# The border from ffn_down to dil_in by halves of tokens, and dil_in's first group with its value columns second

## What is computed

```python
# first block, its end
h = rms_norm(x, g_ffn_pre[l])
x = x + rms_norm(swiglu(h, w_gate_up[l], w_down[l]), g_ffn_post[l])
# second block, its start (rms_norm_2 is the same norm)
h = rms_norm_2(x, mixer_norm[layer])
proj = (h @ w_in).reshape(B, S, ATTN_N_GROUPS, 3, ATTN_HEADS_PER_GROUP, ATTN_HEAD_DIM)
for g, (window, dilation) in enumerate(ATTN_GROUPS):
    q = rms_norm_2(proj[:, :, g, 0], q_gain[g]) * scale
    k = rms_norm_2(proj[:, :, g, 1], k_gain[g])
    o, lse = dilated_window_attention(q, k, proj[:, :, g, 2], window, dilation)
```

## Time and profile before

| | us |
|---|---|
| median of three runs | 1457.39 |
| lowest and highest | 1456.97, 1458.7 |
| the profiled execution, device time | 1458.71 |
| the profiled execution, first to last instruction | 1456.9 |

### The profile page before, as it was taken

How to read it: one execution, slowest core, us unless ns; L and a number is a source line. 1 busy time by engine, 2 the same in 40 slices (tenths; PEclk the granted TensorE clock), 3 DMA queues, 4 the chain that set the end, 5 groups by cost and what they waited for, 6 DMA issues and landing times.

```text
span 1456.9 us, 22944 instructions
## 1 busy us (share of the span) xinstructions
PE 1443.8 (99%) x8638; PEld 1223.7 (84%) x8638; DVE 958.1 (66%) x1475; ACT 641.8 (44%) x1000; POOL 345.9 (24%) x313
## 2 busy tenths in 40 slices
PE   9999999999999999999999999999999999999999
PEld 6888779898899888888999788888888888888787
DVE  6524673566628665547877787737666867767878
ACT  6222675453345322222555542433665333335554
POOL 0200102020021743543000564555422110110000
PEclk9999999999999999999999999999999999999999
DMA  5622103422034898786745123222203333334543
GB/s 178 199 91 88 58 2 117 145 87 88 1 87 147 285 311 307 283 279 262 259 137 191 58 87 112 91 88 87 60 2 87 86 102 100 86 106 152 197 152 123
DMA packets 170779, 195.91 MB, mean 134 GB/s; under 512 B 8636, under 2 KB 136636, under 8 KB 167876
## 3 DMA queue, kind: packets, MB, share of 16 engines
q1 hardware_dynamic: 164036, 168.49, 36.5%
q0 software_dynamic: 5600, 26.24, 4.6%
q10 hardware_dynamic: 1056, 0.00, 0.0%
HBM read 169.52 MB, written 25.19 MB: 134 GB/s over the span
## 4 chain that ended last, share of the span: by engine, by line
PE 95%; DVE 3%; ACT 1%; issue 0%; DMA 0%; POOL 0%; SPq 0%; POOLq 0%; DVEq 0%; ACTq 0%
PE ps L2510 27%; PE ps L2512 27%; PE ps L2511 27%; PE ps L2963 3%; PE ps L3052 2%; PE ps L3070 1%; PE ps L3150 1%; PE ps L3159 1%; PE ps L2973 1%; PE ps L658 1%; DVE w_lo L2240 1%; ACT w_hi L1492 0%; PE ps L2994 0%; PE ps L3218 0%; PE ps L3219 0%
## 5 line engine op out<-in xcount | busy, mean ns | idle before, releaser
L2510 PE MATMUL ps<-a_hi,w_hi 128*128 128x512 f32 (+2 forms) x1708 | 608.1, 356 | 5.5 <-issue 2.8
L2512 PE MATMUL ps<-a_hi,w_lo 128*128 128x512 f32 (+2 forms) x1708 | 603.1, 353 | 0.0
L2511 PE MATMUL ps<-a_lo,w_hi 128*128 128x512 f32 (+2 forms) x1708 | 602.9, 353 | 0.0
L2510 PEld LDWEIGHTS ps<-a_hi,w_hi 128*128 128x128 f32 (+1 forms) x1708 | 322.9, 189 | 54.3 <-issue 7.0
L2512 PEld LDWEIGHTS ps<-a_hi,w_lo 128*128 128x128 f32 (+1 forms) x1708 | 322.8, 189 | 45.1
L2511 PEld LDWEIGHTS ps<-a_lo,w_hi 128*128 128x128 f32 (+1 forms) x1708 | 322.9, 189 | 44.4 <-issue 0.7
L1124 ACT ACTIVATE w_hi<-raw 128x2048 fp32r<-128x2048 f32 x94 | 179.7, 1912 | 172.4 <-PE ps L2512 172.4
L1702 DVE TENSOR_TENSOR w_lo<-raw,w_hi 128x2048 fp32r<-128x2048 f32 x75 | 176.1, 2348 | 87.5 <-ACT w_hi L1124 87.1
L2211 DVE TENSOR_TENSOR arena<-ps,rstd 128x512 f32<-128x512 f32 x88 | 59.6, 687 | 124.9 <-PE ps L2512 119.8
L2510 PE MATMUL ps<-w_hi,a_hi 128*128 128x512 f32 x346 | 135.6, 392 | 1.7 <-DVE w_lo L2240 1.4
L2512 PE MATMUL ps<-w_hi,a_lo 128*128 128x512 f32 x346 | 134.8, 390 | 0.0
(11 more groups left out here) (290 smaller groups left out, 1782.9 us busy)
## 6 DMA issues: line engine op xcount, KB each, us to landing
raw<-in_w_gate_up SPq DMA_DIRECT2D x44, 512.0 KB, 5.2
raw<-in_ffn_w_up SPq DMA_DIRECT2D x44, 512.0 KB, 4.5
raw<-in_attn_w_in SPq DMA_DIRECT2D x36, 512.0 KB, 4.2
raw<-in_w_in SPq DMA_DIRECT2D x24, 512.0 KB, 4.7
arena<-in_ffn_w_down SPq DMA_DIRECT2D x24, 512.0 KB, 6.0
arena<-in_w_down POOLq DMA_DIRECT2D x22, 512.0 KB, 6.8
sums_dram<-arena POOLq DMA_DIRECT2D x11, 1024.0 KB, 4.2
sums_dram<-arena SPq DMA_DIRECT2D x11, 1024.0 KB, 4.2
```

What stands on the lines that cost most here:

```text
L2510: pe.matmul(dst, s_hi, m_hi, start=start, stop=False, skip_group_check=across)
L2511: pe.matmul(dst, s_hi, m_lo, start=False, stop=False, skip_group_check=across)
L2512: return pe.matmul(dst, s_lo, m_hi, start=False, stop=stop, skip_group_check=across)
```

## The change

**In ffn_down.** The last two steps put their weights into the two halves of slot 1, so slot 0 is free for dil_in after step 25 (before: after step 27); step 27 now waits for step 24, and step 28 for step 26. The norm of the later 256 tokens (half 1) is taken inside the last run: PE sums in front of step 24 (`post_sum(1)`), ACT takes the root behind its work for step 26, DVE inverts in front of its work for step 27 (`factor_of_half`), PE spreads in front of step 25 (`post_spread(1)`), and DVE, ACT and DVE scale, add, round and subtract by feature tile and half (`post_scaled`, `post_hi`, `post_lo`), in 256 columns. POOL adds nothing to x any more. `stay_clocked` is gone.

**At the border.** PE starts with the first two tiles of dil_in for half 1, eight feature tiles of six 256-column matmuls, as each becomes ready; then come two blocks of the values' first chunk for half 1, the two tiles for half 0, and the values' other two blocks (`dil_opening`).

**In dil_in.** The first group's chunks come in the order 0, 4, 5, 1, 2, 3. Its tiles lie in banks 0, 1, 0, 1, 2, 3, 6, 7, so tile 2 needs tile 0's bank and tile 3 tile 1's. The sum of the squares for `mixer_2` and the first two averages move into chunk 5 (`mixer_means`). DVE scales the values between tiles 1 and 2. ACT's list for the first group is written anew.

```diff
-                self.w, self.half = self.g % 2, (c - PAIRS_K) // 2 % 2
+                last_two = c >= DOWN_STEPS - 2
+                self.w = DOWN_0 % 2 if last_two else self.g % 2
+                self.half = c - (DOWN_STEPS - 2) if last_two else (c - PAIRS_K) // 2 % 2
+                self.w_free = c - (2 if c < PAIRS_K + 2 or c == DOWN_STEPS - 1 else 3 if last_two else 4) + 1
...
+        DIL_ORDER = ((0, 4, 5, 1, 2, 3), tuple(range(6)), tuple(range(6)))
...
         def tile_bank(grp, t):
 
-            return (6, 7, 0, 1)[t - 4] if grp == 0 and t >= 4 else t % 4
+            return (0, 1, 0, 1, 2, 3, 6, 7)[t] if grp == 0 else t % 4
...
             def dil_chunk(grp, c):
-                ch = Chunk(G["dil_in"], grp, 6, c)
+                ch = dil_at(grp, c)
                 if ch.first_of_gemm:
                     pool.wait_ge(norms["mixer_2"].added, 3)
                     squares_split(0)
                     return
+                if ch.second_of_gemm:
+                    return
                 split_lo(ch)
-                if ch.second_of_gemm:
+                if grp == 0 and c == 5:
                     squares_split(1)
                 if c < 4:
                     squares_split(8 * grp + 2 * c)
...
+            post_hi(1, 2)
+            ch = Chunk(G["ffn_down"], 0, 2, DOWN_STEPS - 1)
+            act.wait_ge(raw_loaded[ch.next_slot], ch.next_loads)
+            act.wait_ge(tile_done, G["ffn_down"].signal0 + DOWN_STEPS - 3)
+            act.activation(w_hi[:, ch.next_slot, :], raw[:, ch.next_slot, :], ACT.Copy).then_inc(weights_hi, 1)
             act.wait_ge(mask_ready, 10)
+            post_hi(1, 3), post_hi(1, 4)
...
+            post_hi(1, 5)
             split_hi(Chunk(G["dil_in"], 0, 6, 0))
+            post_hi(1, 6), post_hi(1, 7)
+            root_of_half(0)
...
+                if grp == 0:
+                    if c == 0:
+                        square(0), square_top(0), square(1)
+                        split_hi(dil_at(0, 5))
+                        mixer_norm_out()
+                        square_top(1)
+                        root(0)
+                    elif c < 4:
+                        split_hi(ch)
+                        square(2 * c), square_top(2 * c)
+                        root(2 * c - 1)
+                        square(2 * c + 1), square_top(2 * c + 1)
+                        root(2 * c)
+                    return
...
+            def halves_of_residual():
+
+                post_lo(1, 2), post_scaled(1, 3)
+                split_here(Chunk(G["ffn_down"], 0, 2, DOWN_STEPS - 1))
+                for k in range(3, KT):
+                    if k > 3:
+                        post_scaled(1, k)
+                    post_lo(1, k)
+                factor_of_half(0)
+                split_here(Chunk(G["dil_in"], 0, 6, 0))
+                post_scaled(0, 0)
+                for k in range(KT):
+                    if k + 1 < KT:
+                        post_scaled(0, k + 1)
+                    post_lo(0, k)
...
+                elif t.c == RUNS[2] + 4:
+                    post_scaled(1, 0), post_scaled(1, 1), post_lo(1, 0), post_scaled(1, 2), post_lo(1, 1)
+            halves_of_residual()
+            half_sum("mixer_2", KT + 4)
+            split_here(Chunk(G["dil_in"], 0, 6, 1))
...
+                chunk_ready(tiles)
+                half(1)
+                post_spread(0)
+                chunk_ready(values)
+                pe.wait_ge(norms["ffn_post"].sq, 6)
+                value_blocks((2, 3))
+                half(0)
+                value_blocks((0, 1)).then_inc(tile_done, 2)
...
-            summed(norms["ffn_post"], "dil_in")
...
+                    pe.wait_ge(freed["dve"], ch.freed + (j + 1) - (2 if grp == 0 or grp == 1 and c < 2 else 0))
...
-                    elif t >= 1 and not ch.second_of_gemm:
+                    if grp == 0 and t >= 3 or grp and t >= 1 or grp == 1:
                         head_mean(8 * grp + (t - 1), t - 1)
```

More of the change, by code:

```diff
@@ L2840, in seven_products, with post_sum @@
                         pe.sem_inc(tile_done, 1)
+            def post_sum(h):
+                norm = norms["ffn_post"]
+                pe.wait_ge(product_joined, 5)
+                pe.wait_ge(norm.added, CREDIT + (7, 5)[h])
+                blocks = (2 * h, 2 * h + 1)
+                for b in blocks:
+                    last = pe.matmul(ps[:, 4, b:b + 1], square_sum[:, b * 128:(b + 1) * 128], ones[:, 0:1],
+                                     start=b == blocks[0], stop=h == 1, skip_group_check=True)
+                if h == 0:
+                    for f in range(4):
+                        pe.wait_ge(norm.sq, 4 + f // 2)
+                        for b in blocks:
+                            last = pe.matmul(ps[:, 4, b:b + 1], token_squares(1)[:, f, b * 128:b * 128 + 128], ones[:, 0:1],
+                                             start=False, stop=f == 3, skip_group_check=True)
+                last.then_inc(norm.sum, 1)
@@ new lines, in post_spread, with dil_opening, half, value_blocks @@
+            def post_spread(h):
+                norm = norms["ffn_post"]
+                pe.wait_ge(norm.inverse, 2 * (1 - h) + 2)
+                pe.matmul(ps[:, POST_FACTOR[h], 0:256], ones[:, :], diagonal[:, HALVES[h]], start=True, stop=True)\
+                  .then_inc(norm.spread, 1)
+            def dil_opening():
+                tiles, values = dil_at(0, 0), dil_at(0, 4)
+                ready = norms["mixer_2"].ready
+                whi, wlo = weights(tiles.slot, KT)
+                vhi, vlo = weights(values.slot, 4)
+                def half(h):
+                    for k in range(KT):
+                        pe.wait_ge(ready, (1 - h) * KT + k + 1)
+                        for j in range(2):
+                            cols = slice(j * 128, j * 128 + 128)
+                            last = three(ps[:, j, HALVES[h]], (whi[:, k, cols], wlo[:, k, cols]),
+                                         (a_hi[:, k, HALVES[h]], a_lo[:, k, HALVES[h]]), k == 0, k == KT - 1, across=True)
+                            if h == 0 and k == KT - 1:
+                                last.then_inc(tile_done, 1)
+                        if h == 1 and k == 4:
+                            post_sum(0)
+                    return last
+                def value_blocks(blocks):
+                    for b in blocks:
+                        tok = slice(b * 128, b * 128 + 128)
+                        for k in range(4):
+                            last = three(ps[:, value_banks(0)[b], :], (a_hi[:, k, tok], a_lo[:, k, tok]),
+                                         (vhi[:, k, :], vlo[:, k, :]), k == 0, False, across=True)
+                    return last
+                chunk_ready(tiles)
[6 more added lines that the diff above has]
+                value_blocks((0, 1)).then_inc(tile_done, 2)
```

201 lines of the change are left out of this document (96 added, 105 removed).

## The result

The changed kernel takes **1462.96 us** (median of seven runs, 1462.07 to 1463.97) against 1457.78 (seven runs, 1456.97 to 1458.70) for the kernel before: **5.2 us more**, ratio 1.0036 with a 95% interval of 1.0024 to 1.0048. The forecast was 1460.5, slower by 3.1 than the median of three runs that it started from. The profiled execution took 1462.71 with a span of 1460.9, 4.0 more than the one before. The other 1.2 us is a matter of which execution was profiled: the one before was the slowest of its seven, the one after among the faster.

The account below looks back on a forecast made before the run. The prediction took PE, busy 1443.8 of 1456.9 us, as the bound: 7.1 us won at the border, 10.3 lost in two waits (6.2 and 4.1), so +3.1 on 1457.39 gives 1460.5; range 1456.0 to 1465.5.

Parts of the forecast that it names:

- PE's wait before tile 3: First group of dil_in: PE waits 6.2 us for tile 1's bank, as root(1) stands behind tile 2's squares on ACT.
- the values' first matmul: At the border: the value chunk's first matmul comes at 814.65, set by a chain through ACT and DVE.
- One sign: Trace sign at the border: first dil_in matmul near 803.6 and no matmul of dil_in at 0.43 pitch.
- The border's gain: From ffn_down's end through the values' first half: ends at 831.4 where it stood at 838.5, 7.1 us won.
- the sum: Whole change: 7.1 us won, 10.3 lost in two waits; group 0 ends at 891.0 for 887.95, +3.1 us.
- nobody waits for POOL: At the border: POOL no longer adds to x, and nobody waits for it.
- The second wait: Before head_mean(4): PE waits 4.1 us more, for POOL's split at 878.3, behind DVE's values and tile 2's norm.
- Half clock on the path: Rival: half clock once more, in the border's pieces or at tile 6, +6.1 us in all, 1463.5; chance 0.25.
- The skill's rule: Frequent short idles between matmul groups can throttle the clock; the border would run slowly, change costing 6.1 for 3.1.
- The faster rival: Tile 1's bank free in time if root(1) runs before 845.5: both waits vanish, -7.1 us, 1450.3; chance 0.12.

Follow-up runs that it names:

- step 1: Changed kernel with ACT's root(1) moved ahead of the rounding of chunk 2's weights and the squares of tile 2: 1458.73 us, ratio 1.0005.
- step 8: On top of step 7, POOL adds its two pairs of squares only when all of half 0 are there: 1451.06 us, ratio 0.9956.
- step 7: On top of step 6, ACT rounds the second group's second chunk of weights ahead of root(6): 1452.31 us, ratio 0.9963.
- step 9: Changed kernel with 26 matmuls that compute nothing in PE's wait before tile 3: 1465.64 us, ratio 1.0052.
- step 10: On step 5, half 1's first three feature tiles moved behind ffn_down's last split, on DVE and ACT: 1462.30 us, ratio 1.0028.
- step 11: On step 8, four matmuls that compute nothing in PE's 1.0 us wait for dil_in's first weights: 1451.16 us, ratio 0.9954.
- step 4: Changed kernel with root(1) early and ACT's rounding of chunk 3's weights ahead of root(2): 1458.68 us, ratio 1.0005.
- step 2: Changed kernel with only ACT's rounding of chunk 3's weights moved ahead of root(2), root(1) still late: 1465.01 us, ratio 1.0051.
- step 5: On step 4, the second group's first weights also rounded ahead of root(4): 1456.68 us, ratio 0.9994.
- step 6: On step 5, in half 1 DVE scales and adds feature tile k + 1 ahead of post_lo of tile k: 1455.21 us, ratio 0.9984.
- step 12: Border by halves as in step 6, with dil_in's order, banks and lists as in the kernel before: 1460.45 us, ratio 1.0019.

## Why the prediction was right or wrong

**Direction and mechanism held.** PE's wait before tile 3 was forecast at 6.2 and measured 6.24, for root(1) behind tile 2's squares; step 1 took it away by that line alone. On the forecast's clock (the trace's times and 0.40) dil_in began at 803.58 for 803.6, and the values' first matmul came at 814.65 for 814.65, the same to the hundredth, which for durations laid end to end is partly luck. The values ran 858.3 to 870.5 where 856.9 to 869.1 was forecast, and POOL's split ended at 879.7 for 878.3, in the order forecast. One sign failed: no matmul of dil_in at the pitch of half clock. There was half clock at the border and behind tile 3's wait, the second of which the forecast itself expected a few paragraphs earlier.

**The border's gain was mis-sized by 1.15.** Half 0 and the values' first half took 17.9 us (814.25 to 832.15) for the 16.75 of the sum, so the border brought 6.0 and not 7.1. Most of it is one row: DVE's post_lo of 1.52 in place of 0.48, beside POOL's addition. Step 8 took that away, and the same stretch fell from 17.89 us in step 7's profile to 17.06. The sentence that nobody waits for POOL missed this: an instruction of DVE is slower beside POOL's, and PE waits for it.

**The second wait was forecast at 4.1 and measured 0.78.** The forecast priced it with PE at full clock, and said that half clock behind the 6.2 us would use up the spare time. It did: 0.50 over 858 to 864, and tiles 3 to 5 took some 3.3 us more. The sum is not touched, since it goes by POOL's split.

**The sum.** Tile 8 started at 891.75 with one average of 0.46 owed, against 887.76 before. That is +4.45, and with the offset of 0.40 it is +4.85 where the sum had +3.1. Of the 1.8 missing, 1.15 is the border, 0.2 the way from there to POOL's split, 0.25 the way from the split to tile 8, and 0.2 the base: 887.95 is when ACT's wait ended, not when PE went on.

**The median.** The spans differ by 4.0 and not by 4.85 or more because two places that the change doesn't touch favoured the changed kernel's profiled execution: 0.40 us before 696, and a wait near 1370 us that lasted 0.90 where it was 1.43 before. Taken between two points that both traces have, the wait at 696 and head_mean(8), the change costs 4.95 us (695.85 to 903.20 against 696.25 to 898.65), close to the 5.2 of the medians. So the 2 us by which the median misses the forecast are for the most part the terms above. The seven executions of the changed kernel had mean clocks of 0.995 to 0.997, but the time doesn't follow them (0.995 took 1462.07 to 1463.77, 0.997 took 1462.96), and in the profile the largest part of the loss of clock is the hidden stretch at tile 3.

**Half clock on the path** (+6.1) was not seen in the changed kernel. At the border the forecast took 0 for it; there was half clock (0.72 over 808 to 814), but it ended before the values' matmuls, which came on time. In its other executions it was not traced. Steps 9 and 10 show that it costs some 3 us where nothing hides it, step 11 about 1.

**The skill's rule.** The profile of the changed kernel does show a throttled border, as the Trainium skill (TensorE: Matmul & The Clock Gate, "A second HAM failure mode: psum-queue depth-cycling") would have it: 0.72 over 808 to 814, with no wait of PE over 1.0 us before it. The forecast's reason against it, that only an idle stretch of 2.79 us had dropped the clock, did not carry over. Whether short idles did it is not shown either: step 11 had the slow stretch without them, and steps 4, 7 and 8 had them without the slow stretch. The cost the rule would have given, 3 us, was not paid there in the profiled execution.

**The faster rival** named its point rightly, root(1) before 845.5, and its price wrongly: with the root early (step 1) the values ended 6.2 us earlier, but the next links of ACT's list took over, 3.61, 3.29 and 2.32 us in turn. It took four edits of that list (those of steps 1, 2, 5 and 7) until PE had no wait over 0.31 us left in the group.

## What to carry to other kernels

When a chunk of work is moved forward on a bound engine, write down for every other engine what its own list now puts ahead of what: the loss here sat in one ACT list, where work that could run at once (a root, a rounding of weights) stood behind work that had to wait. A backlog on one engine (here 12.2 us of values on DVE) did no harm once nothing that another engine needs was queued behind an instruction that waits for it. So issue weight preparation ahead of the step that depends on the backlog, at each link and not only at the first. A wait of the matmul engine can cost more than its own length, since half clock may follow it (step 10: about 4 us, and 3 more in six of eight executions); whether that is paid depends on what stands behind it.

One more, on method: compare two traces from a point ahead of the change. The fourteen profiles, of kernels with the same code up to ffn_down's end, differ by up to 0.8 us at 696 us (695.61 in steps 2 and 5, 696.45 in step 6), and the wait near 1370 us, which no edit touches, lasts from 0.90 to 2.12. Differences of 1 to 2 us between medians or spans are easily credited to an edit that did not make them.

## What the runs showed of the hardware

- Whether a wait drops the clock differs from one execution to the next. A wait of 3.61 us left the clock at 1.00 in step 1's profile (873.08) and one of 3.60 halved it in step 9's (879.88); one of 2.32 left it at 1.00 in step 5's (895.31) and one of 2.35 was followed by 0.72 over 894 to 900 in step 6's. The eleven executions of step 4, with a wait of 3.29 us, scattered from 1456.5 to 1461.3 with mean clocks from 1.000 down to 0.996; the five of step 8, without such a wait, from 1450.3 to 1451.6.
- Fillers in a wait can cost time: with 26 matmuls the median rose by 2.7 us (step 9), as the wait moved to a place where the clock's fall was paid.
- DVE is slowed by POOL: a `scalar_tensor_tensor` of 256 columns with two SBUF operands took 1.52 us beside a POOL addition for 0.48 alone, and ended 0.3 us behind it (823.58, 823.29); a split of 2048 columns took 3.39 for 2.29 (steps 8 and 12). A reduction of 2048 columns with one SBUF operand was hardly touched (3.91 for 3.89).
- DVE's scaling (`tensor_scalar` from PSUM) of 32 partitions by 512 takes 0.76 us (12.22 for sixteen), where one of 128 partitions by 512 takes 0.75 in the later groups; quarter-height instructions save nothing.
